# A two-layer hybrid decoder trunk on one core: own semaphore for the weights' low parts, a first unit in two parts, and another order of steps

## The chip, the cores and the metric

The kernel runs on one core of one Trainium2 chip. The metric is device time in microseconds (us) of one execution, as a median over runs. PE is the matrix engine (TensorE), PEld its weight loads, DVE the vector engine, ACT the scalar engine, POOL GpSimd, SP the sync engine, which here only issues DMAs.

## The reference, cut to what matters

Two layers are applied to x (512 tokens, 1024 channels, f32); all parameters are per layer.

```python
for l in range(DEPTH):                        # 2
    h = rms_norm(x, mix_norm[l]); z = h @ w_in[l]
    c_q, c_kv, k_r, hq, hf, hi, hg, guv, gates = split_sizes(z, IN_SIZES)
    y_a = mla(...) @ w_branch_a[l]            # 8 heads, causal softmax, rotary part of 32
    y_b = hgrn2(hq, hf, hi, hg, ...) @ w_branch_b[l]   # 4 heads, gated linear recurrence in chunks of 64
    y_c = gmlp(guv, ...) @ w_branch_c[l]      # gelu, layer norm, causal token mixing in chunks of 128
    x = x + (g_a * y_a + g_b * y_b + g_c * y_c) @ w_mix_out[l]
    x = x + cross_attn(rms_norm(x, xa_norm[l]), rms_norm(mem, mem_norm[l]), ...)   # 4 heads, 256 memory rows
    gt, up = jnp.split(rms_norm(x, ffn_norm[l]) @ ffn_w_in[l], 2, axis=-1)
    x = x + (silu(gt) * up) @ ffn_w_out[l]
return rms_norm(x, final_norm)
```

## The kernel before

The residual stream lives transposed in SBUF (`xT`, 8 tiles of 128 channels by 512 tokens). Every large product is computed from high and low parts: an operand f32 is split into `hi` (rounded to fp32r) and `lo = f32 - hi`, and a product is three matmuls, hi·hi, lo·hi and hi·lo (lines 565, 566 and 567, in `product`).

The work is cut into **units**, each one tile of weights (up to 128x1024) and the products with it: `("u", name, j)`. A unit from the hidden state has 8 slices of the contraction, so 24 matmuls; the units of `w_branch_*` (`y_a`, `y_b`, `y_c`) have 12. SP loads a unit's weights into one of 3 `raw` slots, ACT copies them to `wH` (line 928, `split`), DVE subtracts to `wL` (line 1330, `weight_low`), each of 4 slots, and PE multiplies. ACT and DVE prepare the unit that stands four places on whenever they come to a unit.

The order of all work is a list written out by hand, `PLAN`, made by `plan()`; each engine walks through it (PE by `PLAN`, ACT and DVE by `READERS_PLAN`, which is the same but for two norms set one place earlier) and emits its share of each step. So each engine's queue holds its work in that order, and an instruction that waits holds up all behind it. Completion is told by one counting semaphore per engine; `after(l, step)` is the count at which a step is done, `own(l, "vector")` waits until all earlier counted work of the engine itself is done. The loop over the two layers is a loop on the engines (`Fori`); its first units are prepared at the top of the body.

Steps which the change and the prediction touch:

- the first unit `gv 0` waits for both parts of its weights and, slice by slice, for the normalised input (`mix_h_ready`); `low_x` makes the low part of one slice of the hidden state, `add_square` sums its squares; `("norm", which)` sums over channels on PE (line 652), and `rh` = 1/rms is made by a root on ACT and a reciprocal on DVE.
- gMLP: `gv`, `gu` units, `gm_sum`, `gm_mean`, `gm_var` (sums over channels on PE, line 666), `gm_vt`, `gm_mix`.
- HGRN, per head h: gate chain `f_1` (three DVE operations), `f_2` (four ACT operations with two table loads), `f_3` (two DVE operations, the second makes `hlf`); `hg_lf` transposes `hlf` (line 687) and splits it (`lfH`, `lfL`); `hg_exp` (two halves) is the matmul of cumulated decays (lines 705, 706) and its exponentials; `hg_attn` the products inside chunks with mask and reduction on DVE (lines 1509, 1513); `hg_state` the states `st` (line 1528); `hg_out` the output (line 751); `hg_norm`, `hg_ob` the head's norm (reciprocal of 512 columns, line 1533) and its split (`obH` on ACT line 1120, `obL` on DVE line 1298).
- MLA, per head h: `q`, `k` units, `q_swap` (two DMAs on ACT's queue that swap the rotary halves), `q_rot`, `mla_s` scores (line 784) and softmax, `mla_t` transposes, `mla_v` (line 807).
- cross attention: `x_s`, `x_t`, `x_v` (line 861), then the units `xo`; `lb` makes the lower bounds of the gates from four small exponentials and logarithms on ACT and some thirty tiny DVE operations.

Of the kernel before, what the change touches and what calls it, by code (L numbers as in the profile page):

```python
# [19 lines left out]
F32 = mybir.dt.float32  # L20
# [7 lines left out]
P = 128  # L28
# [44 lines left out]
TABLES = 5  # L73
# [31 lines left out]
def plan():  # L105

    u = lambda name, j=0: ("u", name, j)
    p = [u("gv", 0), ("norm", "mix"), ("angle", 0), u("gv", 1), ("lb",), u("gv", 2), ("angle", 1), u("gv", 3), u("hf", 0), ("gm_sum",), ("gm_ws",)]
    p += [u("gu", 0), ("gm_mean",), u("gu", 1), ("gm_var",), ("f_1", 0), u("gu", 2), ("f_2", 0), ("angle", 2), u("gu", 3), ("angle", 3)]
    p += [u("hi", 0), ("f_3", 0), ("gm_vt",), ("angle", 4), u("hq", 0), ("sin",), ("gm_mix",), u("hg", 0), ("hg_vt", 0)]  # L110
    for h in range(HG):
        n = h + 1
        more = n < HG
        nxt = [u("hq", n), u("hf", n), u("hi", n), u("hg", n)] if more else [u("cq", 0), u("cq", 1), u("cq", 2), u("gate_b", 0)]
        p += [("hg_lf", h), u("gate_c", 2 * h)]
        p += [("hg_exp", h, 0), nxt[0], u("y_c", 2 * h), ("hg_attn", h, 0), u("gate_c", 2 * h + 1), ("hg_state", h, 0)]
        p += ([("hg_norm", h - 1)] if h else []) + [("hg_exp", h, 1), nxt[1], ("hg_out", h, 0)] + ([("hg_ob", h - 1)] if h else [])
        p += [u("y_c", 2 * h + 1)] + ([("f_1", n)] if more else [])
        p += [("hg_attn", h, 1), nxt[2], ("hg_state", h, 1)] + ([("f_2", n)] if more else []) + [nxt[3], ("hg_out", h, 1)]
        p += [("f_3", n), ("hg_vt", n)] if more else []  # L120
    p += [("cq_split",), u("ckv", 0), ("hg_norm", HG - 1), ("norm_q",), u("ckv", 1), ("hg_ob", HG - 1), u("kr"), ("kr_swap",), u("q", 0), ("norm_kv",)]
    p += [("kr_rot",), ("q_swap", 0), u("k", 0), ("q_rot", 0), u("v"), u("gate_b", 1)]
# [80 lines left out]
def build(nc, a, out, known):  # L203
# [7 lines left out]
    with ExitStack() as ctx:  # L211
# [140 lines left out]
        obL = at("obL", RB + 4, [P, 4, T], F32R)  # L352
        hvT = spare
# [44 lines left out]
        red, kk = (at("red0", W + 9, [P, T]), at("red1", W + 10, [P, T])), at("turns", W + 21, [P, T])  # L398
# [15 lines left out]


# [41 lines left out]
        def _(sp):  # L457
# [52 lines left out]
        def _(pe):  # L510
# [38 lines left out]
            def unit(l, name, j):  # L549
# [4 lines left out]
                pe.wait_ge(*after(l, "lo", n))  # L554
# [1218 lines left out]
```

## Time and profile before

| | us |
|---|---|
| median of 3 runs | 2273.79 (2273.67 to 2275.33) |
| the profiled execution's own time | 2276.36 |
| its span, first to last instruction | 2274.6 |
| busy: PE, DVE, ACT, POOL | 2206.3, 1352.5, 1001.4, 9.2 |

The span is what the profile shows instruction by instruction; the profiled execution took 1.8 us more than its span. PE is busy 97% of it. A matmul's end is modelled and overlaps the next one's start, so a stretch without waits counts as fully busy.

### The profile page before, as it was taken

How to read it: one execution, taken by the hardware profiler on the slowest of the kernel's cores; microseconds unless marked ns; L12 is line 12 of the kernel's file. 1: busy time of each engine (PE TensorE's matmuls, PEld its weight loads, DVE VectorE, ACT ScalarE, POOL GpSimd, SP SyncE). 2: the span in 40 equal slices, each digit the busy share in tenths (PEclk: the TensorE clock that was granted, in tenths of full speed). 3: DMA queues.
4: the chain of work that ended last, by engine and by line, in shares of the span. 5: the costliest groups of instructions: out<-in, count | busy, mean ns of one | idle time of the engine just before them, and what ended most of it. 6: DMA issues, size and time to landing. Idle time of an engine off the chain costs nothing.

```text
span 2274.6 us, 31655 instructions
## 1 busy us (share of the span) xinstructions
PE 2206.3 (97%) x10429; PEld 1791.3 (79%) x10429; DVE 1352.5 (59%) x2101; ACT 1001.4 (44%) x1455; POOL 9.2 (0%) x12
## 2 busy tenths in 40 slices
PE   6999999999999999999989999999999999999998
PEld 5787786667888888888868887766688888888886
DVE  7867777665565544443378677866665555444432
ACT  5655644444344423232355565444444443323222
POOL 1000000000000000000000000000000000000000
PEclk9999999999999999999999999999999999999999
DMA  5222221233333233333342222122343323333331
GB/s 162 75 66 66 66 58 48 57 78 112 109 118 102 82 100 97 100 91 96 86 114 75 66 65 59 41 61 58 96 116 104 115 88 97 98 93 102 93 95 63
DMA packets 368094, 197.09 MB, mean 87 GB/s; under 512 B 24268, under 2 KB 361528, under 8 KB 367928
## 3 DMA queue, kind: packets, MB, share of 16 engines
q1 hardware_dynamic: 362008, 185.68, 29.3%
q10 hardware_dynamic: 5920, 9.31, 1.3%
q8 instruction: 90, 1.47, 0.3%
q14 instruction: 76, 0.62, 0.1%
HBM read 191.68 MB, written 2.10 MB: 85 GB/s over the span
## 4 chain that ended last, share of the span: by engine, by line
PE 81%; DVE 10%; issue 4%; ACT 3%; DMA 1%; ACTq 0%; DVEq 0%; SPq 0%
PE PS L565 23%; PE PS L567 23%; PE PS L566 23%; PE PS L784 2%; DVE wL L1330 2%; PE PS L807 2%; PE PS L725 1%; DVE attn L1513 1%; DVE mprod L1509 1%; PE PS L794 1%; PE PS L624 1%; PE PS L622 1%; PE PS L623 1%; DVE rstd L1533 1%; ACT wH L928 1%
## 5 line engine op out<-in xcount | busy, mean ns | idle before, releaser
L928 ACT ACTIVATE wH<-raw 128x1024 fp32r<-128x1024 f32 (+4 forms) x406 | 383.6, 946 | 1004.1 <-PE PS L567 900.5
L565 PE MATMUL PS<-hH,wH 128*128 128x512 f32 x1696 | 675.6, 398 | 18.2 <-DVE wL L1330 14.6
L566 PE MATMUL PS<-hL,wH 128*128 128x512 f32 x1696 | 663.0, 391 | 0.0
L567 PE MATMUL PS<-hH,wL 128*128 128x512 f32 x1696 | 663.0, 391 | 0.0
L1330 DVE TENSOR_TENSOR wL<-raw,wH 128x1024 fp32r<-128x1024 f32 (+4 forms) x406 | 436.9, 1077 | 174.9 <-ACT wH L928 172.4
L565 PEld LDWEIGHTS PS<-hH,wH 128*128 128x128 f32 x1696 | 320.1, 189 | 90.8 <-issue 17.2
L566 PEld LDWEIGHTS PS<-hL,wH 128*128 128x128 f32 x1696 | 320.2, 189 | 68.0 <-issue 3.2
L567 PEld LDWEIGHTS PS<-hH,wL 128*128 128x128 f32 x1696 | 319.6, 188 | 68.3
L1293 DVE TENSOR_TENSOR gate<-PS,rh 128x512 f32<-128x512 f32 x92 | 63.6, 691 | 151.3 <-PE PS L567 150.3
L567 PE MATMUL PS<-fH,wL 128*128 128x512 f32 x352 | 136.9, 389 | 0.0
L565 PE MATMUL PS<-fH,wH 128*128 128x512 f32 x352 | 136.9, 389 | 0.0
L566 PE MATMUL PS<-fL,wH 128*128 128x512 f32 x352 | 136.9, 389 | 0.0
L1276 DVE TENSOR_TENSOR xT<-xT,PS 128x512 f32<-128x512 f32 x48 | 33.0, 687 | 139.6 <-PE PS L567 139.6
L1293 DVE TENSOR_TENSOR fm<-PS,rh 128x512 f32<-128x512 f32 x44 | 30.4, 691 | 135.8 <-PE PS L567 135.7
L567 PEld LDWEIGHTS PS<-fH,wL 128*128 128x128 f32 x352 | 66.1, 188 | 13.8
L565 PEld LDWEIGHTS PS<-fH,wH 128*128 128x128 f32 x352 | 66.1, 188 | 13.7
L566 PEld LDWEIGHTS PS<-fL,wH 128*128 128x128 f32 x352 | 66.1, 188 | 13.7
L1513 DVE TENSOR_REDUCE attn<-mprod 128x128 f32<-128x896 f32 x32 | 56.3, 1760 | 1.1
L784 PE MATMUL PS<-mk,mq 96*128 96x128 f32 (+3 forms) x128 | 48.3, 500 | 5.2 <-DVE mq L1570 3.4
L565 PE MATMUL PS<-mgH,wH 128*128 128x512 f32 x128 | 49.8, 389 | 0.0
L566 PE MATMUL PS<-mgL,wH 128*128 128x512 f32 x128 | 49.8, 389 | 0.0
L567 PE MATMUL PS<-mgH,wL 128*128 128x512 f32 x128 | 49.8, 389 | 0.0
(340 smaller groups left out, 3252.3 us busy)
## 6 DMA issues: line engine op xcount, KB each, us to landing
raw<-in_w_in SPq DMA_DIRECT2D x106, 512.0 KB, 3.9
raw<-in_ffn_w_in SPq DMA_DIRECT2D x88, 512.0 KB, 3.8
raw<-in_xa_w_kv SPq DMA_DIRECT2D x32, 512.0 KB, 4.0
raw<-in_ffn_w_out SPq DMA_DIRECT2D x32, 512.0 KB, 4.0
raw<-in_w_mix_out SPq DMA_DIRECT2D x16, 512.0 KB, 4.3
raw<-in_xa_w_q SPq DMA_DIRECT2D x16, 512.0 KB, 4.0
raw<-in_xa_w_o SPq DMA_DIRECT2D x16, 512.0 KB, 4.1
raw<-in_ffn_w_out SPq DMA_DIRECT2D x16, 384.0 KB, 3.3
```

Source lines behind the costliest of these rows:

```text
L565: nc.tensor.matmul(o, w0, xh(k0 + k), start=(first and k == 0), stop=False)
L566: nc.tensor.matmul(o, w0, xl(k0 + k), start=False, stop=False)
L567: ins = nc.tensor.matmul(o, w1, xh(k0 + k), start=False, stop=(last and k == kts - 1))
L622: nc.tensor.matmul(xv_banks[i], xh, w0, start=(kk_ == 0), stop=False)
L623: nc.tensor.matmul(xv_banks[i], xh, w1, start=False, stop=False)
L784: nc.tensor.matmul(o[:, 0:n], mq[0:96, h % 2, i * P:n], mk[0:96, h % 2, 0:n], start=True, stop=False)
L807: ins = nc.tensor.matmul(oa_bank[r, kb * P:T], mv[:, kb, h * VD:(h + 1) * VD], mpt[:, PT_OFF[kb]:PT_OFF[kb] + n], start=(kb == 0), stop=(k ...
L928: nc.scalar.activation(wH[:, PLACE[n] % NS, 0:w], raw[:, PLACE[n] % NR, 0:w], ACT.Copy).then_inc(*did("scalar", "hi", n))
L1276: V.tensor_tensor(xT[:, j, :], xT[:, j, :], bank(*step) if name != "fo" else bank("fo", j), ALU.add)\
L1293: V.tensor_tensor(dst, src, scale, ALU.mult).then_inc(*did("vector", *me))
L1330: V.tensor_tensor(wL[:, s, 0:w], raw[:, r, 0:w], wH[:, s, 0:w].bitcast(F32), ALU.subtract).then_inc(*did("vector", "lo", n))
L1513: V.tensor_reduce(attn[:, i, :], mprod[:].rearrange("p n t -> p t n"), AX.X, ALU.add)\
```

## The change: what it does

1. `wL` signals an own semaphore, `weights_low`, in place of DVE's counter. SP, which waits for it before it reloads a `raw` slot, finds the first three slots free from the start. Four of the five constant tables are loaded from SP's queue ahead of the first weights instead of from ACT's; the mask is loaded within the loop, with a semaphore of its own.
2. The first unit of a layer runs hi·hi and lo·hi of seven slices with a wait for the high part alone, then hi·lo of seven, then the eighth slice. ACT and DVE make the last slice of the hidden state between their first and second weight tile instead of behind the fourth. The order of the norm is: `gv 0`, `gv 1`, norm, `gv 2`; `lb` stands first of all.
3. `gm_var` stands one unit later, `gm_vt` two; `f_1`, `f_2`, `f_3` of a head earlier (the unit `hf` before `hq`, `f_3` ahead of the last unit before `hg_out`); `hg_lf` and `hg_vt` of head 0 ahead of `gm_mix`.
4. `hg_norm` has an `rstd` of its own for head 3, and head 3's norm and split stand later; the MLA norm of k and v makes its 512-column factor by four matmuls that broadcast the 4-column reciprocal (`rkv`) instead of by a sum and a reciprocal of 512 columns; the division by the row sums of the softmax is a step of its own (`mla_n`), behind the unit `q` of the next head; `y_b` stands behind `q_swap`.
5. The first nine matmuls of `y_a 0` and `y_a 1` are issued around the last `mla_v`, the first twelve of `xo 0` and `xo 1` around the last two `x_v` (`begin`); in the last product `fo`, the low part and square of a slice are done one unit earlier.

```diff
-    p = [u("gv", 0), ("norm", "mix"), ("angle", 0), u("gv", 1), ("lb",), u("gv", 2), ("angle", 1), u("gv", 3), u("hf", 0), ("gm_sum",), ("gm_ws",)]
-    p += [u("gu", 0), ("gm_mean",), u("gu", 1), ("gm_var",), ("f_1", 0), u("gu", 2), ("f_2", 0), ("angle", 2), u("gu", 3), ("angle", 3)]
+    p = [("lb",), u("gv", 0), u("gv", 1), ("norm", "mix"), u("gv", 2), u("gv", 3), ("angle", 0), u("hf", 0), ("gm_sum",), ("gm_ws",)]
+    p += [u("gu", 0), ("gm_mean",), u("gu", 1), ("f_1", 0), u("gu", 2), ("gm_var",), ("f_2", 0), ("angle", 1), u("gu", 3), ("f_3", 0), ("angle", 2)]
...
+        p += [("hg_attn", h, 0), u("gate_c", 2 * h + 1), ("hg_state", h, 0)] + ([("f_1", n)] if more else [])
+        p += ([("hg_norm", h - 1)] if h else []) + [("hg_exp", h, 1), nxt[1], ("hg_out", h, 0)] + ([("f_2", n)] if more else [])
+        p += ([("hg_ob", h - 1)] if h else []) + [u("y_c", 2 * h + 1)]
+        p += [("hg_attn", h, 1), nxt[2], ("hg_state", h, 1)] + ([("f_3", n)] if more else []) + [nxt[3], ("hg_out", h, 1)]
...
+            p += [u("q", h + 1), ("mla_n", h), ("q_swap", h + 1), u("y_b", h), u("k", h + 1), ("mla_t", h), ("q_rot", h + 1)]
...
+            p += [("mla_n", h), u("y_b", h), u("gate_a", 1), ("mla_t", h), ("begin", "y_a", 0), ("mla_v", h), ("begin", "y_a", 1)]
...
-    p += [u("xv", 5), u("xv", 6), u("xv", 7), ("x_t", 3), ("x_v", 2), ("x_v", 3)]
+    p += [u("xv", 5), u("xv", 6), ("x_t", 3), u("xv", 7), ("begin", "xo", 0), ("x_v", 2), ("x_v", 3), ("begin", "xo", 1)]
...
+            sp.sem_inc(sem("weights_low"), NR)
+            for t, c0 in ((tri[:], C_TRI), (freq, C_FREQ), (identB[:].bitcast(F32), C_IDB), (negB[:].bitcast(F32), C_NEGB)):
+                sp.dma_start(t, a["consts"][:, c0:c0 + t.shape[-1]]).then_inc(sem("tables_in"), 16)
...
+                    if first:
+                        wh = lambda k: wH[:, s, k * m:(k + 1) * m]
+                        for k in range(kts - 1):
+                            pe.wait_ge(sem("mix_h_ready"), l * KT + (k + 1))
+                            nc.tensor.matmul(o, wh(k), hH[:, k, :], start=(k == 0), stop=False)
+                            nc.tensor.matmul(o, wh(k), hL[:, k, :], start=False, stop=False)
+                        pe.wait_ge(*low_done(l, n))
...
+                    elif kind == "rkv":
+                        o = take(l, ("rkv",), ("rkv",))
+                        pe.wait_ge(*after(l, "rkt_r"))
+                        for i in range(TT):
+                            ins = nc.tensor.matmul(o[:, i * P:(i + 1) * P], rkt[:, i:i + 1].broadcast_to([P, P]), ident[:], start=True, stop=True)
...
-                V.tensor_tensor(wL[:, s, 0:w], raw[:, r, 0:w], wH[:, s, 0:w].bitcast(F32), ALU.subtract).then_inc(*did("vector", "lo", n))
+                V.tensor_tensor(wL[:, s, 0:w], raw[:, r, 0:w], wH[:, s, 0:w].bitcast(F32), ALU.subtract).then_inc(sem("weights_low"), 1)
```

ACT's queue in head 1 of HGRN, from the last exponential of the second half's decays (`dec`) to the copy `obH`; before, with `t_97` to `t_99` the temporaries of the gate chain:

```order
L1097 ACTIVATE dec<-PS 128x512
...
L928 ACTIVATE wH<-raw 128x1024
...
L974 ACTIVATE t_97<-t_99 128x512
...
L976 ACTIVATE t_97<-t_97 128x512
...
L978 ACT_TABLE_LOAD
L978 ACTIVATE t_98<-t_97 128x512
...
L1120 ACTIVATE obH<-onrm 128x512
```

The same place on ACT in the change:

```order
L1136 ACTIVATE dec<-PS 128x512
...
L964 ACTIVATE wH<-raw 128x1024
...
L1010 ACT_TABLE_LOAD
L1010 ACTIVATE hq<-hq 128x512
...
L1092 ACT_TABLE_LOAD
L1092 ACTIVATE hk<-t_100 128x512
...
L1094 ACTIVATE t_97<-t_99,lbc 128x512
...
L1096 ACTIVATE t_97<-t_97 128x512
...
L1098 ACT_TABLE_LOAD
L1098 ACTIVATE t_98<-t_97 128x512
...
L1159 ACTIVATE obH<-onrm 128x512
```

Ahead of `obH` the three operations on the new `hf` have gone, and the silu of `hq` and all of `f_2` (lines 1092 to 1098) have come.

PE's queue around the last `mla_v` (rows on `mpt`), before:

```order
L794 MATMUL PS<-ident,mp 128x128 x2
...
L794 MATMUL PS<-ident,mp 128x128
...
L807 MATMUL PS<-mpt,mv 64x512
...
L807 MATMUL PS<-mpt,mv 64x384
...
L565 MATMUL PS<-oaH,wH 128x512
```

The same place on PE in the change:

```order
L833 MATMUL PS<-ident,mp 128x128
...
L577 MATMUL PS<-oaH,wH 128x512
L578 MATMUL PS<-oaL,wH 128x512
L579 MATMUL PS<-oaH,wL 128x512
...
L846 MATMUL PS<-mpt,mv 64x512
...
L577 MATMUL PS<-oaH,wH 128x512
```

Nine matmuls on `oaH` and `oaL` now stand between the transposes and `mla_v`, and nine more behind it.

## Rows read from the trace of the kernel before

**Rows 1.** the page, section 1: busy us (share of the span) and instructions
```profile
...
PE 2206.3 (97%) x10429; PEld 1791.3 (79%) x10429; DVE 1352.5 (59%) x2101; ACT 1001.4 (44%) x1455; POOL 9.2 (0%) x12
```

**Rows 2.** waits of PE by total: us in total, times, longest us
```profile
...
PE PS L565 <- DVE wL L1330: 14.6, 2, 9.3
PE PS L751 <- DVE st L1528: 8.2, 6, 1.8
...
PE PS L687 <- DVE hlf L1477: 5.7, 5, 1.7
PE PS L861 <- DVE xvL L1298: 4.2, 2, 2.1
PE PS L807 <- ACT mpt L1166: 4.1, 2, 2.1
PE PS L666 <- DVE gsum L1434: 4.0, 2, 2.0
PE PS L784 <- DVE mq L1570: 3.4, 3, 1.9
...
PE PS L784 <- DVE wL L1330: 1.9, 1, 1.9
```

**Rows 3.** mean granted clock of PE over the span
```profile
...
core 0: 2274.6 us, clock 0.988
```

**Rows 4.** windows: us, busy of PE, PEld, DVE, ACT, POOL, PEclk, DMA, GB/s
```profile
...
0.00:30.00 30.00, 12.57 (x51) 10.85 (x52) 16.74 (x19) 16.23 (x22) 9.16 (x12) 0.83 0.71 189
374.00:380.00 6.00, 6.00 (x16) 3.63 (x14) 2.38 (x7) 4.44 (x11) 0.00 (x0) 0.55 0.06 14
800.00:900.00 100.00, 100.00 (x443) 82.81 (x442) 45.92 (x55) 29.60 (x36) 0.00 (x0) 1.00 0.33 95
```

**Rows 5.** timeline, start: start us, us, what, tile, [idle before <-releaser]
```profile
...
17.61 0.58 ACT L904 ACTIVATE xT<-PS 128x512 f32<-128x512 f32 x1
...
19.51 1.28 ACT L928 ACT_TABLE_LOAD   x1 [1.33 <-issue]
20.81 2.95 ACT L928 ACTIVATE wH<-raw 128x1024 fp32r<-128x1024 f32 x3
...
22.82 3.49 DVE L1330 TENSOR_TENSOR wL<-raw,wH 128x1024 fp32r<-128x1024 f32 x3
...
24.29 0.79 PE L565 MATMUL PS<-hH,wH 128*128 128x512 f32 x1 [9.31 <-DVE wL L1330]
```

**Rows 6.** timeline of head 1's second half, layer 0: DVE, then ACT, then PE
```profile
...
192.07 3.35 DVE L1533 RECIPROCAL rstd<-rstd 128x512 f32<-128x512 f32 x1 [0.99 <-ACT rstd L1116]
...
204.66 0.69 DVE L1298 TENSOR_TENSOR obL<-onrm,obH 128x512 fp32r<-128x512 f32 x1 [2.70 <-ACT obH L1120]
...
207.13 0.68 DVE L1462 SCALAR_TENSOR_TENSOR t<-t,t 128x512 f32<-128x512 f32 x1
...
209.09 1.27 DVE L1509 TENSOR_TENSOR mprod<-mask,PS 128x512 f32<-128x512 f32 x2
...
216.53 1.11 DVE L1528 SCALAR_TENSOR_TENSOR st<-st,eb,PS 128x128 f32<-128x128 f32 x3
...
210.27 1.28 ACT L1053 ACT_TABLE_LOAD   x1
...
214.79 0.63 ACT L1059 ACTIVATE t<-t 128x512 f32<-128x512 f32 x1
...
217.69 0.49 PE L751 MATMUL PS<-attn,hvt 128*128 128x128 f32 x2 [1.79 <-DVE st L1528]
```

**Rows 7.** timeline of PE, first decay product of layer 0
```profile
...
110.81 0.49 PE L705 MATMUL PS<-segM,lfH 128*128 128x512 f32 x1 [1.37 <-DVE lfL L1298]
```

**Rows 8.** timeline of DVE before the first MLA head
```profile
...
361.61 3.35 DVE L1552 RECIPROCAL rkv<-rkv 128x512 f32<-128x512 f32 x1
```

**Rows 9.** timeline of DVE, start of layer 1
```profile
...
1144.86 3.50 DVE L1330 TENSOR_TENSOR wL<-raw,wH 128x1024 fp32r<-128x1024 f32 x3 [1.88 <-issue]
```

**Rows 10.** timeline of DVE, end of the program
```profile
...
2263.27 0.69 DVE L1744 TENSOR_TENSOR sqs<-sqs,sq 128x512 f32<-128x512 f32 x1 [0.71 <-ACT sq L1224]
```

More of the change, by code:

```diff
@@ L113, in plan @@
         more = n < HG
[L114 to L122, printed above, removed]
+        nxt = [u("hf", n), u("hq", n), u("hi", n), u("hg", n)] if more else [u("cq", 0), u("cq", 1), u("cq", 2), u("gate_b", 0)]
@@ L552, in unit, with product @@
                 kts, m = shape_of(name, j)
-                pe.wait_ge(*after(l, "lo", n))
-                def product(o, xh, xl, first=True, last=True, key=None, k0=0):
-                    for k in range(kts):
-                        if name == "gv" and j == 0:
-                            pe.wait_ge(sem("mix_h_ready"), l * KT + (k + 1))
-                        elif key:
+                first = (name, j) == UNITS[0]
+                if first:
+                    pe.wait_ge(*after(l, "hi", n))
+                else:
+                    pe.wait_ge(*low_done(l, n))
+                def product(o, xh, xl, first=True, last=True, key=None, k0=0, ks=None):
+                    for k in ks or range(kts):
+                        if key:
                             pe.wait_ge(*after(l, *key(k)))
@@ L568, in product, with in_two @@
                     return ins
+                def in_two(xh, xl, key):
+                    if begin:
+                        return product(take(l, me, ("ev", name, j)), xh, xl, key=key, ks=range(BEGUN[name]))
+                    return product(PS[:, counted["bank"][me], :], xh, xl, key=key, ks=range(BEGUN[name], kts))
                 me = ("u", name, j)
@@ L585, in unit @@
                         key = lambda k: ("o_lo", name[-1], k)
-                    ins = product(take(l, me, ("ev", name, j)), tile(xh), tile(xl), key=key)
+                    ins = in_two(tile(xh), tile(xl), key) if name == "y_a" and j < 2 else product(take(l, me, ("ev", name, j)), tile(xh), tile(xl), key=key)
                 elif name == "q":
@@ L700, in _ @@
                         pe.wait_ge(*after(l, "lfL", h))
+                        if h == 0 and half == 0:
+                            pe.wait_ge(*after(l, "segM"))
                         for i in range(2):
```

154 lines of the change are left out of this document (91 added, 63 removed).

## The prediction

> **What bounds the kernel now.** I read the busy shares first: PE is busy 2206.3 us [rows 1] of a span of 2274.6, so PE bounds it and 68.3 us of idle is all that any reordering can win at full clock. The waits of PE name who ends that idle [rows 2]: DVE's low weights twice (14.6 us, 9.3 of it in the first layer, so 5.3 in the second), the HGRN states 8.2 in six waits, `hlf` 5.7 in five, `xvL` 4.2, `mpt` 4.1, the gMLP sum 4.0, the rotated queries 3.4, and 1.9 more ahead of the same scores that is put down to `wL`. They are short and spread out; each is worth its own length, and only where PE is not handed over to a next wait.
>
> Then the clock. Over the span it was 0.988 of full [rows 3], and as there are two levels, 1.2 and 2.4 GHz, 0.012 x 2 x 2274.6 = 55 us ran at 1.2. The first 30 us show 0.83, which is 10 of them; a stretch from 374 to 380 shows 0.55 with PE busy throughout [rows 4]: it follows the wait for the rotated queries. In steady work 443 matmuls take 100 us [rows 4], 0.226 each, 5.4 for a unit of 24 and 2.0 for nine. So some 44 us outside the start ran at half speed and cost 22 us, mostly behind the waits of rows 2.
>
> **The change part by part.** The sum is made against the profiled execution, 2276.4 us, which stands 2.6 above the median of the runs.
>
> *Start of layer 0.* ACT ends its last copy of x at 18.19, is idle 1.33 before the table load (the five table DMAs are issued there), splits the first weights at 20.81 to 21.86, DVE follows at 22.82, PE starts at 24.29 [rows 5]. Without the DMAs the load starts about 18.45 and the high part is there at 20.8 (18.45 + 1.28 + 1.05); PE needs no more and starts near 21.05. It then has 14 matmuls to run, while DVE, whose queue is unchanged up to there, ends `wL` at 24.05, so it doesn't stop again: 24.29 - 21.05 = 3.2. What hides the four DMAs now is SP's queue behind the x loads; if they delayed the first weights the gain would be 0. I take 3.2.
>
> *Start of layer 1.* The wait is 5.3 [rows 2]. PE's high parts were made long ago; it can run the 14 matmuls (3.2 us) and then meets `wL`, which DVE can't begin before its loop branch is over: it did at 1144.86 after 1.88 of idle put down to nothing [rows 9]. The branch is reached about 0.8 earlier, since the last low part and square now stand a unit ahead, so `wL` ends near 1145.3 and PE stops for about 1.4. Gain 3.9.
>
> *gMLP.* `gm_var` has a unit of 5.4 us in front of it where the wait was 2.0: 4.0 in two layers. The first decay product waited 1.37 in layer 0 [rows 7]; that goes, but the step now stands right behind `gm_mix` and asks for `segM` too, while DVE comes late from the reciprocal and the eight normalisations, which moved back with `gm_var`. Adding up DVE's queue in the new order from rows of the same instructions gives about 2.1 us of waiting in each layer; the bounds are 0 and 4. Net -2.8.
>
> *HGRN.* The unit `hf` and `f_1` to `f_3` come a unit or more earlier, so `hlf` is ready: 5.7 won. But look at DVE's queue in head 1 [rows 6]. It sat idle 2.70 before `obL`, waiting for ACT's `obH`; then came `f_1` (207.13 to 209.09, 1.96), then the attention products, then `st` (ends 217.64), and PE waited 1.79 for it. In the new order `f_1` stands ahead of the reciprocal, which had 0.99 of slack, so it and everything behind it come about 0.8 later; ACT must then do the silu of `hq` and all of `f_2` before `obH`. `f_2` took from 210.27 to 215.42, 5.15. So `obH` ends about 3.4 later, DVE saves 1.96 behind it, and `st` comes 1.4 later; PE itself is some 0.3 later by a wait for the decays of about 0.4. So the wait for `st` grows from 1.8 to 3.0 in heads 1 and 2 of both layers: -1.2 x 4, and -0.4 x 4 for the decays. In head 0 there is no `obH`, but DVE's next low weights stand behind `f_2` in the same way: a new wait of about 0.9 in each layer. Together -8.2. What is queued behind the waiting `hg_out` is PE's whole next head.
>
> *MLA.* The reciprocal of 3.35 [rows 8] leaves the chain before the first head's rotated queries, that of head 3's norm stays but moves back. The waits for scores of head 0 were about 1.9 in each layer, the other 1.5 are head 7's [rows 2]. I expect 0.4 to be left at head 0 (the two swap DMAs are issued behind the rotated key), so +2.9, and the four broadcasting matmuls take some 0.4 less than the sum they replace, +0.8. Head 7: the swaps are issued 12 matmuls of `y_b` earlier, 2.7 us against waits under 1: +1.5. The last `mla_v` waited 2.05 in each layer and has nine matmuls, 2.0 us, in front of it now: +4.1. The last product of cross attention waited 2.1 twice for `xvL` and gets 2.7 us in front; but `x_t 3` now stands ahead of `xv 7`, so ACT copies its result first, and I leave 0.5 each: +3.2. `xq 0`, the norms of `xa` and `ffn` wait for nothing now or then: 0. `mla_n` behind `q`: DVE only fills its own idle with it while ACT makes the exponentials, 0.
>
> *End.* DVE's last sum of squares ran from 2263.27 [rows 10] behind a low part and a sum (about 1.4 together) that are now done a unit before: +1.3.
>
> Sum at full clock: 3.2 + 3.9 + 4.0 - 2.8 + 5.7 - 8.2 + 3.7 + 1.5 + 4.1 + 3.2 + 1.3 = 19.6.
>
> *Clock.* Of the 22 us lost outside the start I expect those behind the waits that go, and 2 to 5 stretches behind the new, longer HGRN waits, at about 1.7 each: 9 left, 13 won. Bounds: 5 (long waits always followed by a slow stretch, longer than before) and 19.
>
> 2276.4 - 19.6 - 13 = 2243.8 for the profiled execution, 2241 for the median.
>
> **A rule against a row.** ACT's table loads in the new chain before `obH`: `f_2` is two loads of 1.28 and four operations of about 0.65, together 5.16, and took 5.15 [rows 6], so there is no room for anything else. The Trainium skill, page ScalarE: Activation LUTs, section What ACT_TABLE_LOAD costs, adds a drain of about 1.38 us to each switch. By that rule three more switches would put `obH` 4.1 later in each of four heads, and the sum would be some 16 us less. The row has no room for a drain, and the sum goes by the row.
>
> **Rivals.**
> - *ACT is later than I add up.* The mechanism of the long `obH` chain, with three switches that each hold ACT 1.4 longer than the load: four waits of 3.0 become 7, 2241 + 16 = 2257. For it: `obH` already ended DVE's longest idle in the head. Against: `f_2` without any gap. The rule above is this rival. Chance 0.06.
> - *The waits come back one step on.* `lb`, about 6.5 us of small DVE and ACT operations, now stands ahead of the reciprocal `rh`, and so ahead of the fifth unit's `wL`; my margin there is only 1 to 2.4 us. If it is used up, 2 to 4 us each layer are lost, and with them a slow stretch: 2241 + 10 = 2251. Chance 0.14.
> - *The HGRN chain has slack that I don't see*, DVE takes it up, the waits for `st` stay at 1.8 or go, and the clock stays up: 2241 - 8 - 6 = 2227. For it: DVE is only 59% busy. Chance 0.18.
> - *Slower.* `f_2` ahead of `obH` again, as one mechanism: the change wins 19.6 + 8.2 + 13 = 41 us elsewhere, so each of the four heads would have to lose another 10 us, which takes PE at 1.2 GHz for 20 us in each. One wait of some 5 us would have to keep the clock down for as long as four units. From there on it is slower than before: 2280. Against: after 1.8 to 2.1 us of wait the slow stretches were a few us. Chance 0.03.
> - *The change does little*: most waits of rows 2 end by something else at the same time, and only the start, `mla_v` and `x_v` are won: 2262. Chance 0.07.
>
> **How the numbers follow.** My forecast, 2241 us, has 0.52, with its own range of 2233 to 2249. The range that should hold 8 in 10 leaves out the slower case, most of "does little" and part of the late-ACT one, and reaches to the case with slack: 2226 to 2258. A change within 0.2% (4.5 us), about what a measurement of this kernel can tell from none, needs "does little" to go to its end: 0.02. Slower by more than that 0.03, faster 0.95.
>
> **What would show it.** Right: the list of PE's waits without `gsum`, `mpt`, `hlf`, with `wL` at about 1.5 us in one wait behind 14 matmuls; waits for `st` at about 3 us in heads 1 and 2, ended by `obL` behind `obH` on ACT; PE's first unit at 21.0; mean clock about 0.992. Wrong: a wait of PE for `wL` of the fifth unit behind `lb`; `obH` not behind a busy ACT; many slow stretches left; or the first weights landing after 19 us because SP issues tables ahead of them.

## The result and the profile after

| | us |
|---|---|
| before, median of 4 runs | 2274.56 (2273.67 to 2275.35) |
| the change, median of 4 runs | 2243.68 (2240.72 to 2245.19) |
| ratio, 95% interval | 0.9863 (0.9846 to 0.988) |
| the change's profiled execution, own time and span | 2240.72 and 2238.9 |

The change is 30.9 us faster; 2241 had been forecast, inside 2226 to 2258. The profiled executions lie at the ends of the two spreads: 2240.72 is the fastest of its four runs, and 2276.36, before, is above all four of its own. So the profiles differ by 35.7 us where the medians differ by 30.9. First the page of the changed kernel, section 1, which answers to [rows 1]:

```profile
PE 2195.5 (98%) x10441; PEld 1785.5 (80%) x10441; DVE 1341.1 (60%) x2099; ACT 995.3 (44%) x1451; POOL 9.2 (0%) x12
```

The span fell by 35.7 us (2274.6 to 2238.9). PE's idle, span less busy, fell by 24.9 (68.3 to 43.4), and PE's busy time by 10.8, although its profile has 12 matmul records more (the eight broadcasting matmuls of the two layers have two records each, and the two sums that they replace had two each). The second part is the clock. Its mean over the span, which answers to [rows 3], and windows, which answer to [rows 4] (us, busy of PE, PEld, DVE, ACT, POOL, PEclk, DMA, GB/s):

```profile
core 0: 2238.9 us, clock 0.995
```
```profile
0.00:30.00 30.00, 17.00 (x64) 14.21 (x65) 18.45 (x21) 16.97 (x23) 9.17 (x12) 0.89 0.65 170
...
213.00:217.00 4.00, 4.00 (x19) 3.67 (x19) 2.60 (x4) 2.20 (x4) 0.00 (x0) 0.57 0.27 53
272.00:276.00 4.00, 4.00 (x28) 3.70 (x29) 2.94 (x5) 2.09 (x4) 0.00 (x0) 1.00 0.24 70
1230.00:1237.00 7.00, 5.70 (x13) 4.45 (x14) 6.79 (x18) 3.98 (x6) 0.00 (x0) 0.54 0.30 75
...
374.00:380.00 6.00, 6.00 (x28) 4.58 (x26) 4.83 (x10) 0.99 (x3) 0.00 (x0) 1.00 0.46 130
```

From 213 to 217 PE ran 19 matmuls, from 272 to 276, at the same place of the next head, 28: one stretch at 1.2 GHz, one at 2.4, behind waits of the same 2.41 us. Between the start and the end of the program only two slow stretches are left, where the kernel before had nine. Each of those nine began during a wait of PE of 1.7 to 5.3 us or at most 1.3 us behind one.

PE's waits by total in the changed kernel (us in total, times, longest us), which answer to [rows 2]:

```profile
PE PS L784 <- DVE st L1571: 10.5, 6, 2.4
PE PS L544 <- DMA xin<-in_x: 7.8, 2, 5.6
PE PS L601 <- ACT wH L964: 5.2, 1, 5.2
PE PS L577 <- DVE gate L1333: 3.4, 2, 1.7
PE PS L738 <- DVE segM L1457: 2.1, 2, 1.0
PE PS L605 <- DVE wL L1370: 1.4, 1, 1.4
PE PS L577 <- DVE st L1571: 1.4, 6, 0.2
PE PS L738 <- DVE mprod L1552: 1.4, 2, 0.7
PE PS L784 <- DVE onrm L1578: 1.4, 4, 0.3
...
PE PS L900 <- DVE xvL L1338: 0.5, 2, 0.2
PE PS L920 <- DVE sqs L1796: 0.4, 1, 0.4
```

`hlf`, `mpt`, `gsum` and `mq` are gone, 17.2 us, and the 1.9 ahead of the scores that was put down to `wL`; the first units' wait for `wL` fell from 14.6 to 1.4, with 5.2 for `wH` in its place at the start. But the wait for `st` (now line 784, `hg_out`) grew from 8.2 to 10.5, and three rows stand where none stood: for `mprod` and `gate` in head 0, and four short ones for `onrm` (0.3 each). One row of the kernel before that was not among [rows 2] is needed beside `PE PS L577 <- DVE st`:

```profile
PE PS L565 <- DVE st L1528: 3.0, 6, 0.5
```

The start of the program, which answers to [rows 5], ACT, DVE and PE of the changed kernel (start, us, what, [idle before <-releaser]):

```profile
17.96 1.28 ACT L964 ACT_TABLE_LOAD   x1
19.26 1.06 ACT L964 ACTIVATE wH<-raw 128x1024 fp32r<-128x1024 f32 x1
...
22.59 1.23 DVE L1370 TENSOR_TENSOR wL<-raw,wH 128x1024 fp32r<-128x1024 f32 x1
...
20.54 0.79 PE L601 MATMUL PS<-hH,wH 128*128 128x512 f32 x1 [5.16 <-ACT wH L964]
```

The second half of head 1 in the changed kernel, which answers to [rows 6]:

```profile
195.47 1.28 ACT L1092 ACT_TABLE_LOAD   x1
...
199.98 0.63 ACT L1098 ACTIVATE t<-t 128x512 f32<-128x512 f32 x1
200.52 0.61 ACT L1159 ACTIVATE obH<-onrm 128x512 fp32r<-128x512 f32 x1
201.04 0.62 ACT L964 ACTIVATE wH<-raw 128x512 fp32r<-128x512 f32 x1
...
201.17 0.69 DVE L1338 TENSOR_TENSOR obL<-onrm,obH 128x512 fp32r<-128x512 f32 x1 [5.25 <-ACT obH L1159]
...
202.50 0.68 DVE L1370 TENSOR_TENSOR wL<-raw,wH 128x512 fp32r<-128x512 f32 x1
...
210.91 1.11 DVE L1571 SCALAR_TENSOR_TENSOR st<-st,eb,PS 128x128 f32<-128x128 f32 x3
...
212.08 0.49 PE L784 MATMUL PS<-attn,hvt 128*128 128x128 f32 x2 [2.41 <-DVE st L1571]
```

This is the chain that the prediction drew: ACT makes all of `f_2` and only then `obH`, DVE idles 5.25 us for it, and everything behind comes late. The unit's `wH` stands behind `f_2` as well, which the prediction had named for head 0 alone.

### The profile page after: what moved, and what is told of

The parts are those of the page before. It is cut to its first block, busy times and chain, and to the rows that moved or that the text cites. A ratio compares the mean times of both kernels' runs of the same rounds, so it can differ in the third digit from the quotient of the medians.

```text
span 2238.9 us, 31689 instructions
## 1 busy us (share of the span) xinstructions
PE 2195.5 (98%) x10441; PEld 1785.5 (80%) x10441; DVE 1341.1 (60%) x2099; ACT 995.3 (44%) x1451; POOL 9.2 (0%) x12
## 4 chain that ended last, share of the span: by engine, by line
PE 85%; DVE 7%; issue 4%; ACT 3%; DMA 0%; DVEq 0%; ACTq 0%; SPq 0%
PE PS L577 24%; PE PS L579 24%; PE PS L578 24%; PE PS L823 2%; PE PS L846 2%; PE PS L758 1%; DVE attn L1556 1%; DVE rstd L1576 1%; DVE mprod L1552 1%; DVE dec L1538 1%; PE PS L833 1%; PE PS L652 1%; PE PS L654 1%; PE PS L653 1%; ACT wH L964 1%
## 5 line engine op out<-in xcount | busy, mean ns | idle before, releaser
L577 PE MATMUL PS<-hH,wH 128*128 128x512 f32 (+1 forms) x1680 | 666.8, 397 | 4.8 <-DVE gate L1333 3.4
L579 PE MATMUL PS<-hH,wL 128*128 128x512 f32 (+1 forms) x1680 | 656.0, 390 | 0.0
L578 PE MATMUL PS<-hL,wH 128*128 128x512 f32 (+1 forms) x1680 | 655.7, 390 | 0.0
L577 PEld LDWEIGHTS PS<-hH,wH 128*128 128x128 f32 (+1 forms) x1680 | 316.1, 188 | 76.6 <-DVE gate L1333 4.3
L578 PEld LDWEIGHTS PS<-hL,wH 128*128 128x128 f32 (+1 forms) x1680 | 316.2, 188 | 67.1 <-issue 2.9
L579 PEld LDWEIGHTS PS<-hH,wL 128*128 128x128 f32 (+1 forms) x1680 | 315.8, 188 | 67.4
L577 PE MATMUL PS<-fH,wH 128*128 128x512 f32 x352 | 136.9, 389 | 0.0
L577 PEld LDWEIGHTS PS<-fH,wH 128*128 128x128 f32 x352 | 66.1, 188 | 13.7
L579 PEld LDWEIGHTS PS<-fH,wL 128*128 128x128 f32 x352 | 66.1, 188 | 13.6
L577 PE MATMUL PS<-mgH,wH 128*128 128x512 f32 x128 | 49.8, 389 | 0.0
L577 PE MATMUL PS<-xoH,wH 128*128 128x512 f32 x128 | 49.8, 389 | 0.0
```

The costliest lines, as they stand in the source:

```text
L577: nc.tensor.matmul(o, w0, xh(k0 + k), start=(first and k == 0), stop=False)
L578: nc.tensor.matmul(o, w0, xl(k0 + k), start=False, stop=False)
L579: ins = nc.tensor.matmul(o, w1, xh(k0 + k), start=False, stop=(last and k == kts - 1))
```

## The experiments

My theory: PE's own waits and the clock stretches behind them are all that moves; each part of the change is worth the waits it takes away, and HGRN's new order, with `f_2` ahead of ACT's other work, gives some of it back. Rivals: the clock has nothing to do with the waits; or the new order of HGRN wins. All runs, with PE's idle (span less busy) of the profiled one; the ratio is to the runs of before on the same chip, whose medians were 2275.19 (`ob_first` to `filled`), 2274.34 (`no_begin` to `best1`) and 2275.45 (`after_again` to `best2`):

| kernel | median (range), us | ratio (95%) | idle of PE |
|---|---|---|---|
| `ob_first` | 2235.84 (2235.0 to 2236.09) | 0.9827 (0.9814 to 0.9841) | 40.4 |
| `f2_later` | 2227.64 (2227.13 to 2227.91) | 0.9792 (0.9778 to 0.9805) | 33.9 |
| `head0_old` | 2236.84 (2235.15 to 2243.83) | 0.984 (0.9823 to 0.9856) | 42.5 |
| `filled` | 2237.53 (2237.14 to 2239.36) | 0.9837 (0.9823 to 0.985) | 33.9 |
| `no_begin` | 2253.57 (2253.18 to 2260.29) | 0.9908 (0.9893 to 0.9923) | 52.6 |
| `mla_start_old` | 2246.46 (2246.03 to 2248.66) | 0.988 (0.9865 to 0.9896) | 47.1 |
| `hgrn_old` | 2238.64 (2236.25 to 2240.92) | 0.9839 (0.9826 to 0.9853) | 41.4 |
| `best1` | 2221.88 (2219.91 to 2222.66) | 0.9765 (0.9752 to 0.9779) | 30.0 |
| `after_again` | 2242.16 (2238.99 to 2244.34) | 0.9854 (0.9839 to 0.9869) | 44.2 |
| `first_waits` | 2248.66 (2246.87 to 2251.22) | 0.9886 (0.9871 to 0.9901) | 50.5 |
| `tables_act` | 2242.34 (2239.55 to 2245.51) | 0.9855 (0.984 to 0.987) | 44.4 |
| `best2` | 2217.59 (2217.14 to 2217.65) | 0.9747 (0.9734 to 0.976) | 27.9 |

The changed kernel as it is, once more beside the last group:

> The changed kernel itself, unchanged, on the chip and in the rounds of the other kernels of this group, since terms of 3 to 5 us hang on its median and its first four runs spread over 4.5 us. Theory (whether a slow stretch follows one of the four 2.41 us waits changes from run to run): 2238 to 2246 with a median of 2241 to 2244. If the median is at 2238 or less, undoing HGRN's order (2238.6) gained nothing, and undoing the start of MLA (2246.5) costs 8, not 3.

Its four runs gave 2242.16, where the theory had it; differences below are against this median. All eight runs of the changed kernel lie between 2238.99 and 2245.19. The changed kernel ran again in the last group alone, so the first two groups are set against it across chips. The ratio's intervals of `ob_first`, `head0_old`, `filled`, `mla_start_old` and `hgrn_old` overlap that of the changed kernel, so their times count only together with the ranges of the runs and with the traces.

### What is late in HGRN: `obH`, or ACT's whole queue

```diff
-        ... ("hg_out", h, 0)] + ([("f_2", n)] if more else [])
-        p += ([("hg_ob", h - 1)] if h else []) + [u("y_c", 2 * h + 1)]
+        ... ("hg_out", h, 0)] + ([("hg_ob", h - 1)] if h else [])                       # ob_first
+        p += ([("f_2", n)] if more else []) + [u("y_c", 2 * h + 1)]
+        ... ("hg_out", h, 0)]                                                           # f2_later
+        p += ([("hg_ob", h - 1)] if h else []) + [u("y_c", 2 * h + 1)] + ([("f_2", n)] if more else [])
```

> The changed kernel with one step moved: in HGRN heads 1 to 3 the split of the previous head's output (obH on ACT, obL on DVE) stands ahead of f_2 again, so that ACT makes obH at once instead of behind four operations and two table loads. In the changed kernel obL starts behind 5.25 us of idle of DVE for obH, and PE then waits 2.41 us for the states in heads 1 and 2 of both layers. Theory A (obH alone is what is late): the four waits go, 9.6 us, and with them the slow-clock stretches behind them, 2230 to 2234. Theory B (ACT's whole queue is late: the next unit's high part wH stands behind f_2 in either order, and DVE's low part for it stands ahead of the attention products): DVE's low part starts at wH's end, 201.7 instead of 202.5, so each wait shrinks only from 2.4 to about 1.6, 3.2 us in all: 2240 to 2241. I hold B.

> The changed kernel with f_2 of the next head moved behind the split of the previous head's output and behind the unit y_c of the second half, so that ACT does obH and the high part wH of that unit's successor first and f_2 after them. Theory B (obH and wH both stand behind f_2, and DVE's queue with them): ACT ends obH at 196.1 and wH at 196.7 instead of 201.1 and 201.7, DVE's attention products move forward by 4 to 5 us, st is ready some 3 us before PE needs it, and the four waits of 2.4 us go: 9.6 us, and the slow-clock stretches behind them (1.3 to 3 us each where they fell): 2229 to 2234, with less spread between runs. Rival: f_2 now delays the copy of suft (PE's state product wants it at 203.3, it would be there at 202.2) or the next wH, and waits of about 1 us come back there: 2236 to 2239.

DVE in `ob_first`, then ACT and DVE in `f2_later`, same place as above:

```profile
195.91 0.69 DVE L1338 TENSOR_TENSOR obL<-onrm,obH 128x512 fp32r<-128x512 f32 x1
196.64 0.69 DVE L1747 TENSOR_TENSOR acc<-PS,gate 128x512 f32<-128x512 f32 x1
201.60 0.69 DVE L1370 TENSOR_TENSOR wL<-raw,wH 128x512 fp32r<-128x512 f32 x1 [4.27 <-ACT wH L964]
```
```profile
195.16 0.61 ACT L1159 ACTIVATE obH<-onrm 128x512 fp32r<-128x512 f32 x1
195.68 0.62 ACT L964 ACTIVATE wH<-raw 128x512 fp32r<-128x512 f32 x1
196.32 1.28 ACT L1092 ACT_TABLE_LOAD   x1
...
197.14 0.68 DVE L1370 TENSOR_TENSOR wL<-raw,wH 128x512 fp32r<-128x512 f32 x1
...
205.54 1.11 DVE L1571 SCALAR_TENSOR_TENSOR st<-st,eb,PS 128x128 f32<-128x128 f32 x3
```

In `ob_first` `obL` is 5.3 earlier and it helps little: DVE stops again, 4.27 us, for the `wH` that is still behind `f_2`, and the four waits of PE went from 2.41 to 1.6 each (1.64, 1.61, 1.64, 1.59 in the trace), as theory B says. The time fell by 6.3 us where the waits explain 3.2, so the median lies some 4 us below B's 2240 to 2241, with no run above 2236.09. In `f2_later` both copies stand ahead of `f_2`, `st` starts at 205.54 instead of 210.91, and the four waits are gone: 14.5 us faster than the changed kernel for 9.6 us of waits; the median lies 1.4 us below the theory's 2229 to 2234. The rest is the next question.

### The clock: is it the wait?

```diff
                             if i == 0:
+                                if half == 1 and 0 < h < HG - 1:
+                                    for _ in range(20):
+                                        nc.tensor.matmul(ob_bank[:, 2 * P:4 * P], lfH[:, 0, :], segM[:, 0:2 * P], start=True, stop=True)
                                 pe.wait_ge(*after(l, "st", h, half))
```

> The changed kernel with work added and nothing moved: in heads 1 and 2 of both layers, ahead of PE's wait for the states in the second half, 20 matmuls of 256 columns whose result is overwritten, about 2.3 us, which is what PE waits there (2.41). They leave every other engine's work where it is. Theory A (the clock falls because PE stands still): the wait for st shrinks to about 0.1 and the added work takes its place, so the path is as long at full clock, but no slow stretch begins there; the changed kernel's runs of 2240.7 to 2245.2 should gather at their fast end, 2238 to 2241. Theory B (the slow stretches have nothing to do with the waits): median and spread stay, 2243 to 2245, and slow stretches still fall at 213 and 1231.

PE in `filled` at the place of the wait, and windows behind two of the four places and behind head 0's wait:

```profile
209.40 2.55 PE L784 MATMUL PS<-segM,lfH 128*128 128x256 f32 x20
211.97 0.49 PE L787 MATMUL PS<-attn,hvt 128*128 128x128 f32 x2
```
```profile
212.00:218.00 6.00, 6.00 (x37) 5.34 (x38) 3.49 (x5) 2.09 (x4) 0.00 (x0) 1.00 0.47 123
...
1230.00:1233.50 3.50, 3.50 (x10) 2.72 (x9) 3.32 (x8) 3.47 (x6) 0.00 (x0) 0.51 0.40 85
1314.00:1320.00 6.00, 6.00 (x37) 5.35 (x38) 3.49 (x5) 2.09 (x4) 0.00 (x0) 1.00 0.47 122
```

The path is as long as before, `hg_out` starts at 211.97 against 212.08, the other engines' work is unchanged, and yet it is 4.6 us faster than the changed kernel, with four of five runs below the fastest of the changed kernel's eight. The clock was at 2.4 GHz behind all four places in this execution, while the wait left as it was, in head 0 of layer 1, still had its stretch at 0.51. In the seven traces that keep these four waits at 2.4 us each (`after`, `after_again`, `head0_old`, `no_begin`, `mla_start_old`, `first_waits`, `tables_act`), 15 of the 28 have a slow stretch with them; in `filled` it is none of 4, and its five runs all have a mean clock of 0.996, against 0.993 to 0.996 in the changed kernel's eight. So part of what a wait costs is paid behind it. That is theory A, with a median of 0.5 us below its 2238 to 2241. B expected the median and the spread to stay, and neither did. What one stretch costs can be read off two equal paths, from the start of this `hg_out` to the next wait: 37.85 us in the changed kernel (212.08 to 249.93, a stretch of 3.4 us in it), 36.21 in `filled` (211.97 to 248.18, none): 1.6 us.

### Head 0

```diff
-        nxt = [u("hf", n), u("hq", n), ...]
+        nxt = ... if more and h else [u("hq", n), u("hf", n), ...]      # head 0 alone, f_1 behind hg_out(0, 0)
```

> The changed kernel with head 0 of HGRN alone in the old order of units (hq of head 1 before hf, f_1 behind hg_out of the first half), f_3 kept ahead of the last unit. In the changed kernel PE waits 0.68 us for a bank held by mprod and 1.71 us for one held by gate, in each layer, because ACT makes three operations and two table loads for hf of head 1 ahead of wH, for which DVE's queue waits 4.33 us. Theory: with hq first that is one operation and a load, the two waits go, 4.8 us: 2238 to 2240, if hlf of head 1 still comes in time. Rival: f_1 to f_3 of head 1 are then too late, and PE waits 1 to 2 us for hlf in each layer, as before the change (1.74): 2241 to 2244.

PE's waits in `head0_old`, the first row:

```profile
PE PS L784 <- DVE st L1571: 14.6, 8, 2.4
```

The waits for `mprod` and `gate` are gone and `hlf` is in time, so neither the theory nor its rival came whole, and the median of 2236.84 is below both ranges: two waits for `st` took their place (2.05 and 2.03, together 14.6 against 10.5), in head 0's second half. The waits fell by only 0.7 in sum (4.8 won, 4.1 back), the median by 5.3: the rest fits the clock, since no slow stretch followed the new waits in the profiled execution, while one or two follow head 0's waits in seven of the nine profiles that have the new order there (0.54 above, 0.51 in `filled`). One of the five runs, 2243.83 at 0.992, shows that the other outcome remains.

### The output units begun early

```diff
-            p += [..., ("mla_t", h), ("begin", "y_a", 0), ("mla_v", h), ("begin", "y_a", 1)]
+            p += [..., ("mla_t", h), ("mla_v", h)]
-    p += [..., ("begin", "xo", 0), ("x_v", 2), ("x_v", 3), ("begin", "xo", 1)]
+    p += [..., ("x_v", 2), ("x_v", 3)]
```

> The changed kernel without the output units begun early: the four units y_a 0, y_a 1, xo 0 and xo 1 run whole and in their old places, all else as in the change. Theory (the early matmuls fill the wait for mpt and for xvL): the last mla_v waits 2.05 us again in each layer and the last x_v 2.1 instead of 0.24, 7.8 us at full clock, and a slow-clock stretch of 3.4 us follows mla_v in both layers as it did before the change, about 1.5 us of time each: 2253 to 2256. Rival: DVE and ACT had come so much earlier by the rest of the change that the waits are shorter than before, 2246 to 2250.

PE's waits and a window of `no_begin`:

```profile
PE PS L900 <- DVE xvL L1338: 5.9, 2, 3.0
...
PE PS L846 <- ACT mpt L1206: 4.1, 2, 2.1
```
```profile
507.00:511.30 4.30, 4.29 (x10) 1.78 (x11) 0.00 (x0) 0.48 (x2) 0.00 (x0) 0.60 0.38 110
```

11.4 us slower, inside the theory's range. `mla_v` waits 2.05 again with its slow stretch in both layers (0.59 in layer 1); the wait for `xvL` is 2.95 and not 2.1, which fits `x_t 3` standing ahead of `xv 7` now (no run moved it alone), and no slow stretch follows it (1.00 from 724 to 730). 9.5 us of waits and the two stretches behind `mla_v`, some 3, account for it. The profile is of the slowest of the four runs, 2260.29 where the others took 2253.2 to 2253.9; all four HGRN waits of 2.4 us have a slow stretch in it, two of them twice as long.

### The start of MLA

```diff
-                    elif kind == "rkv":            # four broadcasting matmuls, a copy on ACT
+                        V.reciprocal(rkv[:], rkv[:])            # 512 columns, after a sum and a root
-    ... ("norm_kv",), ("hg_norm", HG - 1)] ... ("hg_ob", HG - 1), u("gate_b", 1)]
+    ... u("ckv", 0), ("hg_norm", HG - 1), ("norm_q",), u("ckv", 1), ("hg_ob", HG - 1), u("kr"), ...
```

> The changed kernel with the start of MLA undone: the factor of k is made by a sum, a root and a reciprocal of 512 columns again, head 3's norm and its split stand where they stood, and the four broadcasting matmuls are gone; the order within the heads stays new. Theory (those two reciprocals of 3.35 us are on the chain before head 0's scores): PE waits about 1.9 us for mq in each layer, 3.7 us in all, and one matmul chain of 0.4 less or more; behind that wait the clock was low for 6.8 us in both layers of the kernel before, 3.2 us of time each. So 2250 to 2254, of which over half is clock. Rival: the wait comes back without the slow stretches: 2247 to 2248.

PE and the windows behind the wait in both layers of `mla_start_old`:

```profile
364.74 0.48 PE L819 MATMUL PS<-mk,mq 96*128 96x128 f32 x2 [1.74 <-DVE mq L1608]
```
```profile
364.70:372.30 7.60, 7.56 (x20) 4.23 (x20) 3.73 (x8) 6.25 (x12) 0.00 (x0) 0.55 0.16 44
1472.40:1480.00 7.60, 7.57 (x34) 5.32 (x35) 4.91 (x12) 6.88 (x14) 0.00 (x0) 1.00 0.18 49
```

The waits are back, 3.4 us in two, but undoing this part costs 4.3 us and not 8: the slow stretch came behind one wait (20 matmuls in 7.6 us) and not behind the other (34), and that is below both of my expectations, which had counted two stretches, or a higher base. The run undoes three things at once (the broadcast, the place of head 3's norm, that of its split), so it doesn't say what each is worth.

### HGRN's order

```diff
-        nxt = [u("hf", n), u("hq", n), u("hi", n), u("hg", n)] if more else ...
+        nxt = [u("hq", n), u("hf", n), u("hi", n), u("hg", n)] if more else ...
         # and f_1 behind y_c, f_2 behind hg_state, f_3 behind the last hg_out, as before
```

> The changed kernel with the loop over the HGRN heads in the old order (hq before hf, f_1 behind y_c, f_2 behind the states, f_3 behind the last output product), all else new. Counting PE's idle between 120 and 335 us the two traces have 8.6 us before and 9.0 after in a layer: the order only traded the waits for hlf (3.0) for longer waits for st and a new one in head 0. Theory: within 2 us of the changed kernel at full clock, and as many slow stretches as before, four or five instead of two: 2243 to 2248. Rival (my prediction's terms, -2.5 at full clock for this order against the waits for hlf it takes away): undoing it wins 2 to 3 us, 2240 to 2242.

PE's waits in `hgrn_old`:

```profile
PE PS L783 <- DVE st L1570: 7.9, 6, 1.8
...
PE PS L717 <- DVE hlf L1517: 6.2, 5, 1.7
```

Undoing it was 3.5 us faster (2238.64 against 2242.16). The intervals of the two ratios, taken on two chips, still overlap, so the time alone does not settle it; PE's idle is 2.8 less, and that agrees with the rival's direction and with the prediction's own -2.5; the median is below the rival's 2240 to 2242 too. The theory that the order is neutral was too kind to it.

### The start of the layers

`first_waits` makes the first unit wait for `low_done` before its first matmul; `tables_act` issues the four tables from ACT's queue ahead of the first `wH`.

```diff
-                first = (name, j) == UNITS[0]
-                if first:
-                    pe.wait_ge(*after(l, "hi", n))
-                else:
-                    pe.wait_ge(*low_done(l, n))
+                pe.wait_ge(*low_done(l, n))
...
-                sp.dma_start(t, a["consts"][:, c0:c0 + t.shape[-1]]).then_inc(sem("tables_in"), 16)
+                act.dma_start(t, a["consts"][:, c0:c0 + t.shape[-1]]).then_inc(sem("tables_in"), 16)
```

> The changed kernel whose first unit waits for wL before its first matmul; the matmuls keep their new order, the last slice its new place. Theory (what the two parts bring is the 14 matmuls that run while wL is made): in layer 0 PE starts at 23.8 instead of 20.5, +3.3; in layer 1 it waits 4.6 us in one piece instead of 1.4 behind 14 matmuls, +3.2; and a slow-clock stretch of 3.4 us follows that longer wait as it did before the change, +1.5: 8 us slower than the changed kernel. Rival: at the start of layer 1 most was won by DVE's earlier last slice and not by the 14 matmuls, so that the wait is 2 to 3 us: 4 to 6 us slower.

> The changed kernel with the four constant tables loaded from ACT's queue again, between its last copy of x and the table load ahead of the first wH. Theory: each issue holds ACT, 1.33 us of idle for five before the change, so the first wH is 1.1 us later and nothing takes it up, since PE now waits for wH alone: 1.1 us slower than the changed kernel, within its spread; the profile shows PE's first unit at about 21.6. Rival (SP's queue was in the way of the first weights): no difference at PE's start.

PE in `first_waits` at the start of layer 1, and in `tables_act` at the start of the program:

```profile
1131.32 0.79 PE L597 MATMUL PS<-hH,wH 128*128 128x512 f32 x1 [4.62 <-DVE wL L1366]
```
```profile
21.29 0.79 PE L599 MATMUL PS<-hH,wH 128*128 128x512 f32 x1 [5.99 <-DVE sqs L1306]
```

`first_waits` costs 6.5 us, between the theory (8) and the rival (4 to 6): PE starts at 24.29 instead of 20.70 (`after_again`), and layer 1 waits 4.62 instead of 1.41, 6.8 together, which is the theory's mechanism; the 1.5 for the slow stretch that it added don't show in the median, though the stretch is in the trace, from 1131.3 to 1134.7. `tables_act` shows PE's start 0.6 later (its profile names `sqs`, but `wH` ends at 21.06, 0.2 ahead of PE's start, as in the change) and a median 0.2 higher, which these runs can't tell from nothing. So at the start nearly all comes from the unit in two parts.

### A version from these findings

`best1` joins `f2_later`, `head0_old` and an earlier `sin`; `best2` leaves ACT's part of `sin` where it was and moves only DVE's rounding of `segM`.

```diff
+                        if step[1] == 4:                              # best2, in the step "angle"
+                            dve.wait_ge(sem("seg_in"), l * 16 + 16)
+                            V.tensor_copy(segM[:], seg[:]).then_inc(*did("vector", "segM"))
```

> The changed kernel with three steps moved: f_2 behind the split of the last head's output and the unit y_c (as measured alone, 2227.6), head 0 with hq before hf (alone 2236.8), and the rounding of segM (step sin) one unit earlier, ahead of the unit hg. Theory: the wait for st that head 0's old order gave by itself (2.05 at 153.7) was also one behind f_2 and does not come now; so 2.4 us less in each layer against 2227.6, 0.7 us each for segM (PE then waits for lfL, 0.35 of 1.04 left), and the slow stretches behind head 0 go: 2218 to 2221. Rival: head 0's f_2 is now too late for hlf of head 1, a wait of 1 to 2 us in each layer, 2222 to 2226.

> best1 (2221.9) with its one misstep mended: there the step sin moved as a whole, ACT's sine and cosine came ahead of wH and lfH, and PE waited 1.93 us for lfL in each layer where it had waited 1.04 for segM. Here ACT's part stays where the change has it and only DVE's rounding of segM is moved, behind the last angle, where DVE then idles. Theory: wH and lfH are as early as in the changed kernel, DVE ends lfL at 98.3, PE wants it at 98.0, so 0.3 to 0.4 of waiting is left: 3.1 us less than best1, and the slow stretch at 100.2 (1.3 us) goes: 2217 to 2219. Rival: lfL ends the wait at 1 us as segM did, since the queue on DVE is as long in sum: 2219 to 2221.

PE's waits in `best1`, then in `best2`, and `best2`'s clock between start and end:

```profile
PE PS L738 <- DVE lfL L1338: 3.9, 2, 1.9
```
```profile
PE PS L605 <- DVE wL L1370: 1.3, 1, 1.3
...
PE PS L738 <- DVE lfL L1338: 1.1, 2, 0.5
```
```profile
30.00:2200.00 2170.00, 2163.22 (x10325) 1761.48 (x10324) 1319.27 (x2072) 970.38 (x1418) 0.00 (x0) 1.00 0.31 88
```

`best1`, at 2221.88, missed the theory's 2218 to 2221 by one step: the sine and cosine held `wH` and `lfH`. `best2`, inside the theory's 2217 to 2219, is 24.6 us faster than the change and 57.9 faster than its kernel before. Behind the start no wait above 1.3 us is left, the clock is full to the end, and the five runs differ by 0.5 us, where the changed kernel's eight differ by 6.2.

## Why the prediction was right, step by step

The forecast for the profiled execution was 2243.8, it took 2240.72; the forecast for the median was 2241, it was 2243.68. The terms, from PE's waits before and after:

| term | predicted | in the traces |
|---|---|---|
| start of layer 0 | +3.2 | +3.75 (24.29 to 20.54) |
| start of layer 1 | +3.9 | +3.9 (1.4 left) |
| `gm_var` | +4.0 | +4.0 |
| first decay product of head 0 | -2.8 | -0.7 (1.4 once before, 1.04 twice) |
| HGRN heads, with `hlf` | -2.5 | -1.2 (16.9 to 18.1) |
| MLA, head 0 and its norm | +3.7 | +3.7 (the waits alone) |
| MLA, head 7; last `mla_v` | +1.5; +4.1 | +1.5; +4.1 |
| `x_v`, end | +3.2; +1.3 | +3.7; +1.3 |
| clock | +13 | 10.8 of busy time; 13.6 by half of PE's busy time in the slow stretches (20.9 to 7.3) |

The terms of the waits add up to 24.1 in the traces, of 24.9 us of idle that went, where the forecast had 19.6. `first_waits`, `no_begin`, `mla_start_old` and `hgrn_old` undo the parts that they are named for. No run undoes the later `gm_var`, the order around head 7 or the end alone: for these the waits that are gone from the list are all that shows their worth.

- **Start.** Right, but by the two parts almost alone; the tables, to which I gave the first step of the working, are worth 0.6 us of PE's start and nothing that the median shows. In layer 0 `wL` starts 2.3 after `wH` is there, held by DVE's queue, which the 14 matmuls hide.
- **First decay product.** The step that was mis-sized: I had added up 2.1 us of waiting for DVE's queue in each layer, with `gm_vt` two units later; the plan has it one unit later, behind `hq 0`. The wait came at the step named and for `segM`, 1.04 long: DVE was not as far behind as I had made it, it even idled for `wH` just ahead, as its timeline in the changed kernel shows:

```profile
96.50 1.23 DVE L1370 TENSOR_TENSOR wL<-raw,wH 128x1024 fp32r<-128x1024 f32 x1 [1.36 <-ACT wH L964]
```

- **HGRN.** The mechanism, `obH` behind all of `f_2`, was right; the wait in heads 1 and 2 grew by half of what I had (from 1.8 to 2.41, not to 3.0), and the 0.4 for the decays came as 0.3, for `onrm`. It was incomplete: `wH` stood there too, which `ob_first` separates from `obH`. And head 0's new wait of 0.9, for which I had `f_2`, came as 0.68 and 1.71 through another chain: `hf` ahead of `y_c` puts three operations and two table loads ahead of `wH`. With the old order there (`head0_old`) the wait behind `f_2` does appear, 2.05. That -2.5 lies so near -1.2 is partly luck: -2.4 for `st` where I had -4.8, -4.8 in head 0 where I had -1.8, and 1.6 won ahead of the units, which I had not seen, nearly cancel. In sum the new order of HGRN seems to lose, as `hgrn_old` says, and `f2_later` shows what it gives when it is carried further. It traded the waits for `hlf` and half of those ahead of its units (16.9 us) for 18.1.
- **MLA, `mla_v`, `x_v`, end.** Right in size and place but for head 0 of MLA, whose 3.7 is right by luck: I had 2.9 from the waits, with 0.4 left in each layer, and 0.8 from the four matmuls in place of the sum. Nothing of the waits was left, and the matmuls gained nothing: the sum holds PE from 348.88 to 349.73 in `mla_start_old`, 0.85 us, the broadcast from 351.77 to 352.57 in the change, 0.80. The queue showed that `x_t 3` ahead of `xv 7` makes the wait for `xvL` longer (2.95 in `no_begin`) and the twelve matmuls cover all but 0.24 of it.
- **Clock.** Right in size for the two profiled executions, and too large for the medians: those differ by 4.8 us less (30.9 against 35.7), which is clock if PE's idle is alike in all runs (an estimate), since the profiled run of the change has the highest mean clock of its four, 0.995 against 0.993 to 0.994. So the median landed near 2241 partly by luck, as two errors work against each other: 24.9 us of idle went where I had 19.6, and by the same estimate 6 of the medians' 30.9 us came from PE's busy time where I had 13. `filled` shows that the stretches belong to the waits; the forecast of 2 to 5 stretches behind HGRN's waits fits the two profiles of the changed kernel (two and four, head 0's among them).
- **The rivals.** A drain at table loads: `f_2` in the changed kernel starts at 195.47, and `obH` behind two loads and four operations at 200.52, 5.05 us without a gap. So the 1.38 us that the Trainium skill, page ScalarE: Activation LUTs, section What ACT_TABLE_LOAD costs, adds to each switch does not occur in this chain; the trace disagrees. `lb` ahead of the fifth unit's `wL`: no such wait in the list. Slack in HGRN: not there in the change; only `f2_later` makes it. The change does little, or is slower: the waits for `gsum`, `mpt`, `mq` and `hlf` are gone from the list, with PE's idle 24.9 us less.

## What to carry to other kernels

When a long step on a feeding engine is moved ahead, list everything of that engine that it now holds, the next weights as well as the operand in question; moving one of two victims back took away a third of the waits that moving both did. A short wait of the bounding engine costs more than its length when its clock reacts: here 9.6 us in four waits of 2.4 were worth 14.5. Where a kernel's runs scatter, look for waits that now and then take the clock down; with the last of them gone, the scatter went too.

## What the runs showed of the hardware

Whether a slow stretch follows is not set by the length of the wait alone. The same 2.41 us were followed by 0.57 at 213 and by 1.00 at 272 in one execution; `mla_start_old` had 0.55 behind 1.74 us of waiting in layer 0 and 1.00 behind 1.71 in layer 1; `no_begin` had 1.00 behind 2.95. One of the four waits of 1.6 us in `ob_first` had a slow stretch too (212.8 to 216.2). A slow stretch lasted 3.4 us or twice that, and cost about 1.6 us for each 3.4 (37.85 against 36.21 us above). What decides between two equal waits stays open: no run here varied the instant of a wait by itself.
